# Products with zeros taken out of TensorE's queue between the stages, in the first gate/up and in the compressed branch

## The reference

```python
def modulate(x, shift, scale):
    return rms_norm(x) * (1 + scale[:, None, :]) + shift[:, None, :]

def swiglu(u, w_gate, w_up, w_down):
    return (jax.nn.silu(u @ w_gate) * (u @ w_up)) @ w_down

def compress(k, w1, w2, pe):
...
    blocks = (blocks + pe).reshape(B, G, n_cmp, CMP_BLOCK * d)
    return jax.nn.gelu(blocks @ w1) @ w2
...
    for l in range(DEPTH):
        mod = c_act @ w_ada[l] + b_ada[l]
        sh1, sc1, g1, sh2, sc2, g2, sh3, sc3, g3 = jnp.split(mod, N_MOD, axis=-1)
        x = x + 0.5 * g1[:, None, :] * swiglu(modulate(x, sh1, sc1), ffn1_gate[l], ffn1_up[l], ffn1_down[l])
        x = x + g2[:, None, :] * token_mix(
            modulate(x, sh2, sc2), cos, sin, w_in[l],
...
        x = x + 0.5 * g3[:, None, :] * swiglu(modulate(x, sh3, sc3), ffn2_gate[l], ffn2_up[l], ffn2_down[l])
    return rms_norm(x) * final_norm
```

## Time and profile before

| | |
|---|---|
| median of 3 runs | 1959.36 us (1957.5 to 1962.37) |
| the profiled execution's own time | 1957.13 us |
| its span | 1955.5 us |
| PE, PEld busy | 1812.3 us (93%), 1462.4 us (75%) |
| DVE, ACT busy | 1375.6 us (70%), 953.6 us (49%) |
| mean granted clock of PE | 0.956 |
| products with zeros of 448 and 512 columns | 236 records, 56.9 us busy |

### The profile page before, as it was taken

One profiled execution on the slowest core, in us unless ns is written; L12 is line 12 of the kernel. 1 busy time (PEld: TensorE's weight loads), 2 busy tenths in 40 slices (PEclk: granted clock), 3 DMA queues, 4 the chain that ended last, 5 costly groups with the idle time before them and its releaser, 6 DMA issues.

```text
span 1955.5 us, 25172 instructions
## 1 busy us (share of the span) xinstructions
PE 1812.3 (93%) x8756; PEld 1462.4 (75%) x8772; DVE 1375.6 (70%) x2086; ACT 953.6 (49%) x1427; POOL 47.1 (2%) x92
## 2 busy tenths in 40 slices
PE   6799999999999998999999989998997997999996
PEld 3688777777688767886878767886886675788875
DVE  6877755766766568776567567665677276999886
ACT  4344453654444443444446553444443245777774
POOL 0000000000000000000000000000000000000000
PEclk8899998999999999999989999999998598999998
DMA  9988741224766648884413347664685051999992
GB/s 368 348 307 306 281 144 65 108 92 150 259 252 246 248 174 322 321 306 174 144 65 108 108 173 290 243 244 178 232 326 217 0 193 67 354 352 368 352 352 112
DMA packets 61497, 437.41 MB, mean 224 GB/s; under 512 B 6768, under 2 KB 7280, under 8 KB 9200
## 3 DMA queue, kind: packets, MB, share of 16 engines
q1 hardware_dynamic: 47200, 339.27, 46.6%
q0 software_dynamic: 12672, 92.28, 12.8%
q10 hardware_dynamic: 1552, 4.89, 0.7%
HBM read 435.36 MB, written 1.05 MB: 223 GB/s over the span
## 4 chain that ended last, share of the span: by engine, by line
PE 77%; DVE 14%; ACT 4%; DMA 3%; issue 3%; POOL 0%; ACTq 0%; DVEq 0%; SPq 0%; POOLq 0%
PE bank L1609 22%; PE bank L1610 22%; PE bank L1611 22%; DVE w_lo L886 3%; DMA ada_w<-ada_pairs 2%; DVE ada_w L910 2%; PE bank L1819 2%; PE bank L1836 1%; PE bank L1689 1%; ACT w_hi L485 1%; PE bank L1797 1%; PE bank L1793 1%; PE bank L1799 1%; DVE arena L972 1%; DVE w_lo L893 1%
## 5 line engine op out<-in xcount | busy, mean ns | idle before, releaser
L886 DVE TENSOR_TENSOR w_lo<-raw,w_hi 128x1024 fp32r<-128x1024 f32 x428 | 504.0, 1221 | 258.1 <-ACT w_hi L485 257.1
L485 ACT ACTIVATE w_hi<-raw 128x1024 fp32r<-128x1024 f32 x428 | 428.7, 1053 | 419.1 <-PE bank L1611 413.9
L1609 PE MATMUL bank<-w_hi,uT_hi 128*128 128x512 f32 (+3 forms) x1440 | 561.2, 390 | 22.7 <-DVE uT_lo L1173 11.5
L1610 PE MATMUL bank<-w_lo,uT_hi 128*128 128x512 f32 (+3 forms) x1440 | 547.7, 380 | 0.0
L1611 PE MATMUL bank<-w_hi,uT_lo 128*128 128x512 f32 (+3 forms) x1440 | 546.1, 379 | 0.0
L1609 PEld LDWEIGHTS bank<-w_hi,uT_hi 128*128 128x128 f32 x1440 | 274.4, 191 | 81.6 <-DVE uT_lo L1173 13.5
L1609 PE MATMUL bank<-w_hi,r_arena 128*128 128x512 f32 (+1 forms) x744 | 301.8, 406 | 13.5 <-DVE r_arena L958 5.7
L1611 PEld LDWEIGHTS bank<-w_hi,uT_lo 128*128 128x128 f32 x1440 | 274.2, 190 | 52.0
L1610 PEld LDWEIGHTS bank<-w_lo,uT_hi 128*128 128x128 f32 x1440 | 274.9, 191 | 48.4 <-issue 1.4
L1611 PE MATMUL bank<-w_hi,r_arena 128*128 128x512 f32 (+1 forms) x744 | 297.6, 400 | 0.0
L1610 PE MATMUL bank<-w_lo,r_arena 128*128 128x512 f32 (+1 forms) x744 | 297.6, 400 | 0.0
(11 more groups left out here) (316 smaller groups left out, 1522.7 us busy)
## 6 DMA issues: line engine op xcount, KB each, us to landing
raw<-weight_stream SPq DMA_DIRECT2D x216, 1024.0 KB, 4.9
ada_w<-ada_pairs POOLq DMA_DIRECT2D x88, 1024.0 KB, 5.2
raw<-expert_blocks SPq DMA_DIRECT2D x48, 1024.0 KB, 4.8
ada_w<-expert_blocks SPq DMA_DIRECT2D x32, 1024.0 KB, 4.8
cmpw<-expert_blocks SPq DMA_DIRECT2D x16, 1024.0 KB, 4.8
arena<-ada_pairs SPq DMA_DIRECT2D x5, 1024.0 KB, 13.7
ada_w<-ada_pairs SPq DMA_DIRECT2D x3, 1024.0 KB, 13.2
cmpw<-compress_w ACTq DMA_DIRECT2D x2, 1024.0 KB, 8.3
```

What stands on the lines that cost most here:

```text
L485: act.activation(w_hi[:, b], v, ACT.Copy).then_inc(hi_done, 1)
L886: V.tensor_tensor(w_lo[:, b], v, f32(w_hi[:, b]), ALU.subtract).then_inc(split_done, 1)
L1609: pe.matmul(dst, xh, w_hi[:, off:off + n], start=first, stop=False, skip_group_check=True)
L1610: pe.matmul(dst, xh, w_lo[:, off:off + n], start=False, stop=False, skip_group_check=True)
```

## The change

`keep_warm` and its five calls are removed. Every wait, every other product and every other engine's program stay as they are.

```diff
--- before.py
+++ after.py
@@ -1593,11 +1593,6 @@
 
                 pe.matmul(SPARE[:, 64:65], zeros[:, 0:P], zeros[:, 0:1], start=True, stop=True, skip_group_check=True)
 
-            def keep_warm(n, dst):
-
-                for _ in range(n):
-                    pe.matmul(dst, zeros[:, 0:P], zeros[:, 0:dst.shape[1]], start=True, stop=True, skip_group_check=True)
-
             def need(u, seen, off, n, order=IN_LINE):
                 for h in range(off // HALF_BLK, (off + n - 1) // HALF_BLK + 1):
                     if h not in seen:
@@ -1637,7 +1632,6 @@
                         release(used[j])
 
             def norm(n, q):
-                keep_warm(16, GU[0][:, :])
                 pe.wait_ge(x_ready, 2 * q + 2)
                 for t in range(T):
                     pe.wait_ge(xn_done, 2 * q + t + 1)
@@ -1672,7 +1666,6 @@
                 seen = set()
                 for k in range(KD):
                     if k % 2 == 0:
-                        keep_warm(8, SPARE[:, 0:512])
                         pe.wait_ge(uT_ready, k // 2 + 1)
                     need(0, seen, k * 512, 512, IN_LINE)
                     for t in range(T):
@@ -1704,7 +1697,6 @@
 
                 if nn > 0:
                     pe.wait_ge(mod_ready, nn + 1)
-                    keep_warm(12, GU[0][:, :])
                     gate_up(u0, nn)
                 for b in range(4):
 
@@ -1904,7 +1896,6 @@
                                               proj[:, t, C_KC + (2 * k + g) * DH:C_KC + (2 * k + g + 1) * DH], ident,
                                               start=True, stop=True, skip_group_check=True)
                 m.then_inc(c_psum, 1)
-                keep_warm(16, SPARE[:, 64:512])
                 pe.wait_ge(blocks_ready, l + 1)
                 pe.wait_ge(cqT_ready, l * 3 + 3)
                 carry_waits()
@@ -1926,7 +1917,6 @@
                                       start=True, stop=True, skip_group_check=True)
                 m.then_inc(kvc_psum, 1)
 
-                keep_warm(8, SPARE[:, 64:512])
                 pe.wait_ge(kvc_ready, l + 1)
                 for p in range(2):
                     half = slice(DH * p, DH * p + DH)
```

## The result

The changed kernel takes 1972.88 us (median of five, 1971.58 to 1977.25) against 1957.5 us (five, 1955.44 to 1962.37) for the kernel before, measured in the same rounds: ratio 1.0077, 95% interval 1.0058 to 1.0095. It is slower by 15.4 us. The forecast was 1976 us, its range 1966 to 1986, with 0.87 on slower by over 0.3%.

A forecast was written before the change was run, and what follows sets the result against it. PE was taken to bound the kernel, busy 93% of the span. The terms 2.2 + 3.2 + 0.9 + 0.4 + 5.9 + 5.4 = 18.0 us gave 1975.1 or 1977.4, stated as 1976 us; range 1966 to 1986.

The forecast's parts named there:

- Both effects of the forecast: Where fillers outlasted the wait, the overrun is gained; where PE now stands still, the clock falls and what follows slows.
- Norm before the mixer: Norms at 245 and 907: PE stands 4.0 us, transposes and gates run cold; 1.1 us each, 2.2 us lost.
- Norm before the second FFN: Norms at 482 and 1147: PE stands, then products run cold for 4.2 us; 1.6 us each, 3.2 us lost.
- Norm of 692: Layer 1's norm: transposes keep PE busy, so the clock may return before the products; 0.9 us lost (0 to 1.7).
- Router: Norm of the router at 1615: mostly a chain over VectorE and ScalarE; 0.4 us lost (0 to 1.2).
- Start: First products, from 24.36 us: already cold, the slower second group covered by a wait; 0, at most 1 us.
- Norm at 1355: PE already stands 5.83 us after its fillers and the sixteen transposes already run cold; 0 us.
- Compressed branch: At 305 and 967: small products run at half clock throughout; 5.9 us lost in layer 0, 5.4 in layer 1.
- rival 2: Small products of the compressed branch are not slowed: 12.5 us fall away, 1962.6 or 1965 us; chance 0.03.
- Rival 1: PE's slip is swallowed by waits it does not control, or zeros do not hold the clock; 1957 to 1965; chance 0.09.
- Rival 3: Clock stays down behind the compressed branch, up to the attention: 6 us more per layer, 1988 us; chance 0.06.
- Rival 4: The kernel gets faster; overruns of 1.8 us are the only gains found, over 0.3% needs 5.9; chance 0.03.

The follow-up runs named there:

- e12_norm_32: Kernel before with 32 instead of 16 products with zeros at the head of each norm: 1975.55 against 1956.33 us, ratio 1.0098.
- e9_attn_and_stalls: Kernel before plus zero products ahead of and inside block 2's attention jobs, at the 1355 norm and in the router: 1943.02 against 1955.6 us, ratio 0.9934.
- e6_before_attn: Kernel before plus 14 and 26 zero products before two waits ahead of block 2's attention: 1954.11 against 1957.11 us, ratio 0.9972.
- e7_attn_jobs: e6_before_attn plus eight zero products in each of the four attention jobs, against the kernel before: 1947.52 against 1957.11 us, ratio 0.9948.
- e3_no_ffn: Kernel before without the twelve zero products ahead of gate_up in the three later FFNs: ratio 1.0000.
- e4_no_first: Kernel before without the 4 x 8 zero products in first_gate_up: ratio 1.0001.
- e5_no_norm_ffn: Kernel before without norm's sixteen and ffn's twelve zero products, the compressed branch's and first_gate_up's kept: 1977.77 against 1957.11 us, ratio 1.0103.
- e10_plus_branch: e9_attn_and_stalls plus six zero products amid each small compressed-branch group and eleven instead of eight between: 1941.25 us, ratio 0.9931 to the kernel before.

## Why the prediction was right, point by point

**PE bounds the kernel and a product's time counts only by the wait behind it.** Shown. 56.9 us of PE work went and the kernel became slower. The forecast gave 18 us of busy time back to slower products; it was 33, since products that run cold where PE has slack count as busy too, at no cost to the end (argued; no run separates them). PE stands 4.02 us at 249 where the zeros were. Both effects of the forecast are seen: without the products the clock falls and the kernel is slower, and with 32 at each norm (`e12_norm_32`) the clock is up behind them and their overruns cost.

**Norm before the mixer: 2.2 us forecast, 2.6 measured** (1.6 + 1.0). The mechanism as told: transposes and gates cold, clock full again at the first wide product, 5.6 us after the return, near the upper bound of the 2.6 to 5.9 taken (by its own working, 5.3 and a half, that bound is 5.8).

**Norm before the second FFN: 3.2 forecast, 2.9 measured.** The sum held but a detail of its working did not. It had tile 0's transposes run at once and PE stand 5.1 us before tile 1's. In the trace PE waits 2.64 us for the second half of x, even for tile 0, then 2.46 and 1.65 us. The three stands together did what one was to do.

**Norm of 692: 0.9 forecast (0 to 1.7), 2.1 measured**, 0.7 given back right behind. The term was mis-sized: it had the clock back with the transposes. It was, for five wide products, and was down again from 712.0 to 715.4, eight or nine products of 0.63 us. **Router: 0.4 forecast (0 to 1.2), 1.2 measured** (its four gates took 3.62 us). **Start: 0 and 0.** **Norm at 1355: 0 forecast, -1.6 measured**, which need not be the change's doing (below).

**Compressed branch: 5.9 and 5.4 forecast, 5.6 and 4.8 measured.** The small products were the largest term. L1914 took +3.30 and +2.60 us (3.3 and 2.7 forecast), L1935 +2.5 and +2.7 (3.0 and 3.1: the forecast's 1.91 is L1819's ratio; its own cold time is 6.18 us, not 6.7). In layer 0 the step between the two groups grew by 0.4 us, as forecast, and in layer 1 it shrank by 0.9, the overrun that the forecast had found. The page "TensorE: Matmul & The Clock Gate" of the Trainium skill, section "LDWEIGHTS (loading the stationary operand)", has no clock in a load's time; the runs contradict it for these groups, 3.76 us at full and 7.06 at half clock, one load 192 and 332 ns. This is rival 2, and it fell. The section "Part 4: PE-mode transpose" of the same page of the Trainium skill would have transposes not count; at 1384, with sixteen transposes and nothing else, the clock came back, as the earlier trace rows had shown. The trace doesn't tell whether these fp32 transposes use the mode that the page speaks of.

**Rival 1 (covered)** fell: the late 15.9 us reach the end. **Rival 3 (not back behind the branch)** fell: full clock from 333.2, 4.6 us after the 384-column products began, and in layer 1 from 1005.6, 4.5 us after. **Rival 4** fell, though `e9_attn_and_stalls` shows a faster kernel the other way, with more such products.

**What the sum did not have.** The forecast terms came to 18.0; measured at their places 19.3 (1.6 + 1.0 + 1.5 + 1.5 + 2.1 + 1.2 + 5.6 + 4.8). On top came +0.7, -0.7, -0.8 and +2.4 us elsewhere, where cold stretches lie differently, and 4.8 us came back in three places: at the norm of 1355 the clock is back before the wide products (window 1387.90), where before they ran cold until 1374.4 (-1.6); an adaLN transfer on the chain took 6.00 us instead of 7.63 (-1.6); between 1451 and 1613, where the attention's cold stretch lies, another 1.6. With 0.2 between the marks that is 15.9.

These three need not be the change's doing, since other traces have them without its edits there. The 1.6 us at the norm of 1355 come back in `e6_before_attn` too, whose norms are untouched. The transfer took 5.8 to 6.4 us in eleven of the fourteen traces and 7.3 to 7.6 only in the kernel before, `e6_before_attn` and `e7_attn_jobs`. Between 1451 and 1613 `e3_no_ffn` and `e4_no_first`, which time no different from the kernel before, gain 1.7 and 1.2 us. So the profiled execution of the kernel before had the longer side of all three, by chance as far as is known. That the 18.0 forecast and the 15.9 found agree is therefore in part luck: the terms in the sum came to 19.3, and items that it left out, several of which look like scatter, offset the rest.

**What stays open.** Why the clock falls within L1914's group in one execution and not in another was not settled. Even the untouched kernel had 3.76 and 4.46 us in its two layers, and an edit far ahead changes it. Why the adaLN transfer takes the shorter or the longer time is unknown. And each trace is one execution, while medians of one kernel stand for executions that scatter (`e6_before_attn` from 1938.7 to 1956.6 us): a table by place tells its own execution's story.

## What to carry to other kernels

Products with zeros in a stall are worth having only where what follows is paced by PE, and they must end before the wait does: here 16 covered 4.0 us, and with 32 the kernel was 19 us slower, some 12 of them overruns. Judge them together and by timing, not one by one: what one group gives depends on where the clock falls behind it and on whether the next group begins with the clock up. Look for long half-clock stretches that are busy, not idle; most of the gain of this kernel was there (wide bf16 products ahead of and inside the attention's jobs, 10.2 us), while more of them in other stalls made no difference by themselves.

## What the runs showed of the hardware that was not expected

- A PE that is nearly always busy can stay at half clock: 49.64 of 53.17 us of small fp32 products and transposes at 0.50. In the three kernels with eight 448-column bf16 products of zeros inside it, the clock was back 1.6 to 2.8 us after the first eight began.
- The clock can fall while PE is busy. With the sixteen just run at full clock and a 1.68 us stand behind them, it fell inside 32 small products (5.74 us, `e5_no_norm_ffn`); six bf16 products in their middle did not keep it (1.97, then 3.51 us, `e10_plus_branch`); and before it fell inside wide products at 336.9 us, with PE busy 3.40 of the next 3.40 us.
- A weight load for a small fp32 product takes 192 ns at full and 332 ns at half clock.
- Fillers that begin cold cost nearly double: eight of 448 columns 3.17 us against 1.69.
